# Expert weights split into fp32r parts, moving past stationary tokens, in a hybrid diffusion step

## The reference, cut to what matters

```python
hidden = jax.nn.silu(jnp.einsum('nd,edf->nef', xt, w1)) * jnp.einsum('nd,edf->nef', xt, w3)
y = jnp.einsum('nef,efd->nd', hidden * combine[:, :, None].astype(hidden.dtype), w2)
```

## Time and profile before

| | |
|---|---|
| median of 3 runs | 1863.83 us (1862.94 to 1865.37) |
| the profiled execution's own time | 1864.37 us |
| its span in the trace | 1862.6 us |
| mean granted TensorE clock over the span | 0.91 |
| TensorE matmul busy | 1517.4 us, 81% |
| VectorE busy | 744.2 us, 40% |
| ScalarE busy | 426.4 us, 23% |
| GpSimd busy | 214.2 us, 11% |
| router of layer 0, first instruction to `tok_i` | 739.3 to 760.3 us |
| experts of layer 0, first gather to last down | 760.7 to 996.3 us |
| router of layer 1 | 1522.3 to 1543.2 us |
| experts of layer 1 | 1543.7 to 1806.1 us |

### The profile page before, as it was taken

The page is one execution under the profiler, slowest core; times in us unless marked ns, Lnnn a source line. Parts: engine busy times, 40 slices in busy tenths (PEclk is TensorE's granted clock), DMA queues, the critical chain, the costliest instruction groups (busy, mean ns, idle before and its releaser), DMA issues. The chain is left out here.

```text
span 1862.6 us, 25715 instructions
## 1 busy us (share of the span) xinstructions
PE 1517.4 (81%) x9767; PEld 1213.7 (65%) x9768; DVE 744.2 (40%) x1388; ACT 426.4 (23%) x832; POOL 214.2 (11%) x166
## 2 busy tenths in 40 slices
PE   4699999656899997599993199989997867999970
PEld 1588888555576444477882199987884446777760
DVE  0312122266477343311114835428993752111118
ACT  1311212242343011011112312125552111101113
POOL 1000000112000032100003400010000321100016
PEclk9899999878999998699997599999998977999995
DMA  7576755701000901559994032220006225877763
GB/s 270 176 238 211 242 182 160 171 12 31 1 1 1 296 34 54 170 173 342 354 352 168 23 94 69 80 60 1 1 1 183 102 91 198 280 260 256 269 215 146
DMA packets 190509, 277.82 MB, mean 149 GB/s; under 512 B 12888, under 2 KB 130352, under 8 KB 190416
## 3 DMA queue, kind: packets, MB, share of 16 engines
q1 hardware_dynamic: 180032, 239.15, 39.0%
q0 software_dynamic: 9520, 34.24, 5.3%
q10 hardware_dynamic: 864, 3.15, 0.4%
HBM read 246.90 MB, written 34.85 MB: 151 GB/s over the span
## 5 line engine op out<-in xcount | busy, mean ns | idle before, releaser
L480 PEld LDWEIGHTS psum<-in_parts 128*128 128x128 f32 x3360 | 411.3, 191 | 59.2 <-issue 59.2
L480 PE MATMUL psum<-in_parts 128*128 128x258 f32 (+1 forms) x3360 | 421.2, 286 | 25.3 <-PEq L322 25.3
L773 PE MATMUL psum<-layer 128*128 128x512 f32 x400 | 173.7, 594 | 2.7 <-PEq L698 2.7
L1777 PEld LDWEIGHTS psum<-layer 128*128 128x128 f32 x1280 | 145.7, 192 | 15.2 <-issue 7.6
L1777 PE MATMUL psum<-layer 128*128 128x128 f32 x1280 | 146.5, 275 | 6.7 <-DVE layer L1983 6.7
L1777 PEld LDWEIGHTS psum<-layer,arena 128*128 128x128 f32 x1152 | 137.9, 200 | 13.2 <-issue 6.7
L1777 PE MATMUL psum<-layer,arena 128*128 128x128 f32 x1152 | 138.6, 284 | 5.3 <-DVE layer L1983 3.6
L773 PEld LDWEIGHTS psum<-layer 128*128 128x128 f32 x400 | 75.8, 191 | 95.2 <-issue 95.2
L566 DVE COPY arena<-psum 128x258 f32<-128x258 f32 (+1 forms) x70 | 29.7, 425 | 240.8 <-PE psum L480 240.8
L1168 PE MATMUL psum<-layer 128*128 128x320 f32 (+1 forms) x384 | 114.2, 434 | 5.0 <-PEq L1358 1.7
L1265 ACT ACTIVATE layer<-psum,layer 128x640 f32<-128x640 f32 (+1 forms) x120 | 84.3, 705 | 118.5 <-DVE layer L1211 118.5
(11 more groups left out here) (298 smaller groups left out, 1872.7 us busy)
## 6 DMA issues: line engine op xcount, KB each, us to landing
arena<-in_moe_w SPq DMA_DIRECT2D x48, 1024.0 KB, 9.3
layer<-in_moe_w SPq DMA_DIRECT2D x48, 1024.0 KB, 8.7
in<-in_ada_w SPq DMA_DIRECT2D x40, 1024.0 KB, 5.2
y_rows<-layer SPq DMA_DIRECT2D x64, 256.0 KB, 8.5
in<-in_ev_w_in SPq DMA_DIRECT2D x15, 1032.0 KB, 7.6
in<-in_od_w_in SPq DMA_DIRECT2D x11, 1024.0 KB, 5.1
start<-in_ada_w SPq DMA_DIRECT2D x8, 1024.0 KB, 16.6
arena<-mod_rows SPq DMA_DIRECT2D x16, 512.0 KB, 7.7
```

The costliest lines, as they stand in the source:

```text
L480: last = T.matmul(bank(g % W_BANKS)[:, 0:cw], a, b[:, k], start=(k == 0 and m == 0), stop=(k == KD - 1 and m == 2))
L773: last = T.matmul(bank(g % 4), feats[k][:, t * P:(t + 1) * P], wout[:, k, j * BANK:(j + 1) * BANK], start=(k == 0), stop=(k == kt - 1))
L1777: last = T.matmul(dst[:, (2 * f + m) * P:(2 * f + m + 1) * P], weights[m][:, k, f * P:(f + 1) * P], xT[:, k, :], start=(k == 0), stop=(k = ...
```

## The change

The host stores w1 and w3 of an expert beside each other and by partition, so each of the 128 partitions is one run of 16 KB, and w2 as one run of 8 KB. There are three slots for the arriving weights; SP loads the w1/w3 of expert e+3 (in two halves) once up(e) has ended, and w2 of e+3 behind the store of e. Each weight is split: ScalarE copies the high part, rounded to fp32r, to a place of its own; the low part is written over the raw words, by VectorE for w1/w3 and by GpSimd for w2. Turned tokens are split in the same way, ScalarE for the high part and VectorE for the low part, out of PSUM.

In `up` the tokens are stationary and 512 columns of w1 and w3 together move; for each of the eight k there are three products, high by high, high by low and low by high: 24 matmuls into bank 2. The hidden values then have tokens on the partitions, so after silu and the multiplication TensorE turns them (`turn_h`, two transposes), ScalarE and VectorE split them, and `down` is 12 matmuls of 512 columns. The tokens of a further chunk are turned and split one ahead, in two halves through bank 3, and the chunk uses the split weights of its expert. The loop body holds six experts instead of two.

Expert 0 is prepared in `router`: ScalarE makes three high parts (before and behind its two exponentials), and GpSimd three low parts of 128x2048. `router` also loads the weights of experts 1 and 2, where it loaded those of expert 1. The token lists have two more columns, and `experts` starts with three gathers (experts 0 and 1 and the first further chunk), all turned before the first `up`. The four loads for `combine` are issued behind up(13). The arena is allocated in another way, at the same places. The diff is cut to its core: most lines taken away are left out.

```diff
+HK, W13, W2 = KD // 2, 2 * KD * FF, 2 * D
+LOW13_AT = [BIG + 12 * D, R, R + W13]
+LOW2_AT = [BIG + 12 * D + W13, BIG + 12 * D + W13 + W2, R + 2 * W13]
+HIGH13_AT = [BIG + n * W13 for n in range(3)]
+HIGH2_AT = [R + 2 * W13 + W2 + n * W2 for n in range(2)]
+REST = R + 2 * W13 + 3 * W2
...
+def load13(sp, s, w13):
+    for h in range(2):
+        sp.dma_start(raw13(s, h), w13[:, h * HK:(h + 1) * HK]).then_inc(up_in[s][h], 16)
+def load2(sp, s, w2):
+    sp.dma_start(raw2(s), w2).then_inc(dn_in[s], 16)
...
-sp.dma_start(E13[0], I["moe_w1"][i, 0].rearrange("(k p) f -> p k f", p=P)).then_inc(up_in[0], 16)
-sp.dma_start(E13[1], I["moe_w3"][i, 0].rearrange("(k p) f -> p k f", p=P)).then_inc(up_in[0], 16)
-sp.dma_start(E2, I["moe_w2"][i, 0].rearrange("(f p) n -> p f n", p=P)).then_inc(dn_in[0], 16)
+load13(sp, 0, I["moe_w13"][i, 0])
+load2(sp, 0, I["moe_w2"][i, 0])
+load2(sp, 1, I["moe_w2"][i, 1])
...
+    load13(sp, 1, I["moe_w13"][i, 1])
+    load13(sp, 2, I["moe_w13"][i, 2])
+    load2(sp, 2, I["moe_w2"][i, 2])
+@block.gpsimd
+def _(pool):
+    for h in range(2):
+        pool.wait_ge(high_w, h + 1)
+        nc.gpsimd.tensor_tensor(low13(0, h), raw13(0, h), whole(high13(0, h)), ALU.subtract).then_inc(low_w, 1)
+    pool.wait_ge(high_w2, 1)
+    nc.gpsimd.tensor_tensor(low2(0), raw2(0), whole(high2(0)), ALU.subtract).then_inc(low_w2, 1)
...
 @block.scalar
 def _(act):
+    act.wait_ge(up_in[0][0], 16)
+    A.copy(high13(0, 0), raw13(0, 0)).then_inc(high_w, 1)
     act.wait_ge(nm, 1)
     A.activation(pg, pg, ACT.Exp).then_inc(ex, 1)
     act.wait_ge(nm, 2)
     A.activation(pe_, pe_, ACT.Exp).then_inc(ex, 1)
+    act.wait_ge(up_in[0][1], 16)
+    A.copy(high13(0, 1), raw13(0, 1)).then_inc(high_w, 1)
+    act.wait_ge(dn_in[0], 16)
+    A.copy(high2(0), raw2(0)).then_inc(high_w2, 1)
...
-expert(0, 0, True)
-expert(1, 1, True)
-with eng.Fori(1, HALF) as pair:
-    expert(pair * 2, 0, False)
-    expert(pair * 2 + 1, 1, False)
+def one(e, n):
+    expert(e, n % 3, n % 2, (e - n % 3) // 3 if isinstance(e, int) else None)
+one(0, 0)
+with eng.Fori(0, 2) as six:
+    for j in range(1, 7):
+        expert(six * 6 + j, j % 3, j % 2, six * 2 + j // 3)
+for e in range(NE - 3, NE):
+    one(e, e)
...
+def expert(e, s, b, v):
     done = entry(sp, 2, e)
...
+    more = not (isinstance(e, int) and e >= NE - 3)
+    sp.wait_ge(up_s, e + 1)
+    sp.wait_ge(o_up, done)
     if more:
...
+        load13(sp, s, W13S[bass.ds(e + 3, 1)].rearrange("a p k f -> p (a k) f"))
+    if isinstance(e, int) and e == NE - 3:
+        g2, gb = COMBINE
+        for c in range(2):
+            sp.dma_start(g2[:, c, :].rearrange("p (k m) -> p k m", k=KD), mod_row(i, 5, c)).then_inc(g2_in[i], 16)
+        sp.dma_start(gb[:, 0, :], I["ln2_g"][i].partition_broadcast(P)).then_inc(ln2_in[i], 16)
+        sp.dma_start(gb[:, 1, :], I["ln2_b"][i].partition_broadcast(P)).then_inc(ln2_in[i], 16)
...
+sp.wait_ge(y_a, e + 1)
+sp.wait_ge(y_d, e + 1)
+sp.dma_start(chunk_rows(e), yb[:, b, :]).then_inc(y_out[b], 16)
...
     sp.wait_ge(o_y, done)
...
+    load2(sp, s, W2S[bass.ds(e + 3, 1)].rearrange("a p f n -> p (a f) n"))
...
+def gather(row, col, out, done):
+    nc.gpsimd.tensor_copy(rows[:, row:row + 1], tok_i[:, col:col + 1] if isinstance(col, int) else tok_i[:, bass.ds(col, 1)])
     pool.drain()
...
+def expert(e, s, b, v):
+    pool.wait_ge(turned, e * 2 + 2)
+    gather(b, e + 2, xg[:, b, :], xg_in[b])
+    if not last_of(e):
+        pool.wait_ge(high_w2, e + 2)
+        nc.gpsimd.tensor_tensor(low2((s + 1) % 3), raw2((s + 1) % 3), whole(high2(1 - b)),
+                                ALU.subtract).then_inc(low_w2, 1)
+    def chunk(q):
+        pool.wait_ge(o_turned, q * 2 + 2)
+        gather(2, q + (NE + 1), xg_o, o_in)
     further(pool, e, chunk)
...
+for b in range(2):
+    gather(b, b, xg[:, b, :], xg_in[b])
+gather(2, NE, xg_o, o_in)
 loop(pool, expert)
+for b in range(2):
+    pool.wait_ge(xg_in[b], 8 * (NE + 2))
+pool.drain()
 pool.wait_ge(o_out, entry(pool, 2, NE - 1) * 16)
...
+def turn_half(src, h, dst, done):
+    for k in range(HP):
+        last = T.transpose(dst[:, k * P:(k + 1) * P], src[:, (h * HP + k) * P:(h * HP + k + 1) * P], ident)
+    last.then_inc(done, 1)
+def up(s, x_high, x_low, half, done):
     for k in range(KD):
...
+        half(k)
+        high, low = high13(s, k // HP)[:, k % HP], low13(s, k // HP)[:, k % HP]
+        for m, (a, w) in enumerate(((x_high, high), (x_high, low), (x_low, high))):
+            last = T.matmul(bank(2), a[:, k, :], w, start=(k == 0 and m == 0), stop=(k == KD - 1 and m == 2))
+    last.then_inc(done, 1)
+def turn_h(done):
+    for f in range(2):
+        last = T.transpose(bank(2)[:, f * P:(f + 1) * P], gate[:, f * P:(f + 1) * P], ident)
+    last.then_inc(done, 1)
+def down(b0, s, b, low_ready, done):
+    first, second = high2(b), low2(s)
+    for f in range(2):
+        for w in (first, second):
+            for j in range(2):
+                T.matmul(bank(b0 + j), hh[:, f, :], w[:, f, j * BANK:(j + 1) * BANK],
+                         start=(f == 0 and w is first), stop=False)
+    low_ready()
+    for f in range(2):
+        for j in range(2):
+            last = T.matmul(bank(b0 + j), hl[:, f, :], first[:, f, j * BANK:(j + 1) * BANK], start=False, stop=(f == 1))
+    last.then_inc(done, 1)
+def expert(e, s, b, v):
+    def half(k):
+        if k % HP == 0:
+            pe.wait_ge(x_low, e * 2 + (k // HP + 1))
+            pe.wait_ge(low_w, e * 2 + (k // HP + 1))
+    up(s, xh, xl, half, up_s)
+    pe.wait_ge(xg_in[1 - b], (e + (2 + b)) * 8)
+    for h in range(2):
+        turn_half(xg[:, 1 - b, :], h, bank(h), turned)
     pe.wait_ge(hid_s, e + 1)
...
+    turn_h(h_turned)
+    pe.wait_ge(low_w2, e + 1)
+    pe.wait_ge(h_high, e + 1)
+    if not (isinstance(e, int) and e == 0):
         pe.wait_ge(y_a, e + 0)
         pe.wait_ge(y_d, e + 0)
...
+    down(4, s, b, lambda: pe.wait_ge(h_low, e + 1), y_s)
+    def chunk(q):
+        def half(k):
+            if k % HP == 0:
+                pe.wait_ge(o_xl, q * 2 + (k // HP + 1))
+        up(s, xh_o, xl_o, half, o_up)
+        pe.wait_ge(o_in, (q + 2) * 16)
+        turn_half(xg_o, 0, bank(3), o_turned)
         pe.wait_ge(o_hid, q + 1)
...
+        turn_h(o_ht)
+        pe.wait_ge(o_xl, q * 2 + 3)
+        turn_half(xg_o, 1, bank(3), o_turned)
+        pe.wait_ge(o_hh, q + 1)
+        pe.wait_ge(o_ya, q + 1)
+        pe.wait_ge(o_yd, q + 1)
+        down(6, s, b, lambda: pe.wait_ge(o_hl, q + 1), o_y)
     further(pe, e, chunk)
...
+pe.wait_ge(xg_in[0], 16)
+for h in range(2):
+    turn_half(xg[:, 0, :], h, bank(h), turned)
+pe.wait_ge(o_in, 16)
+turn_half(xg_o, 0, bank(3), o_turned)
+pe.wait_ge(o_xl, 1)
+turn_half(xg_o, 1, bank(3), o_turned)
 loop(pe, expert)
...
+def x_of(e):
+    for h in range(2):
+        act.wait_ge(turned, e * 2 + (h + 1))
+        A.copy(x_half(xh, h), turned_x(h)).then_inc(x_high, 1)
+def x_of_further(q, h):
+    act.wait_ge(o_turned, q * 2 + (h + 1))
+    A.copy(x_half(xh_o, h), turned_x(3)).then_inc(o_xh, 1)
+def split13(e, s, v, h):
+    act.wait_ge(up_in[s][h], (v + 1) * 16)
+    A.copy(high13(s, h), raw13(s, h)).then_inc(high_w, 1)
+def expert(e, s, b, v):
+    s1, v1 = (s + 1) % 3, v + (s == 2)
+    if not last_of(e):
+        split13(e + 1, s1, v1, 0)
+        act.wait_ge(dn_in[s1], (v1 + 1) * 16)
+        A.copy(high2(1 - b), raw2(s1)).then_inc(high_w2, 1)
     act.wait_ge(up_s, e + 1)
...
+    A.activation(gate, bank(2)[:, 0:FF], ACT.Silu).then_inc(silu_s, 1)
+    x_of(e + 1)
+    act.wait_ge(h_turned, e + 1)
+    A.copy(hh, turned_h).then_inc(h_high, 1)
+    if not last_of(e):
+        split13(e + 1, s1, v1, 1)
     act.wait_ge(y_s, e + 1)
...
+    act.wait_ge(y_out[b], (e + (2 - b)) * 8)
     A.copy(yb[:, b, 0:BANK], bank(4)).then_inc(y_a, 1)
...
+    def chunk(q):
         act.wait_ge(o_up, q + 2)
...
+        A.activation(gate, bank(2)[:, 0:FF], ACT.Silu).then_inc(o_silu, 1)
+        x_of_further(q + 1, 0)
+        act.wait_ge(o_ht, q + 1)
+        A.copy(hh, turned_h).then_inc(o_hh, 1)
+        x_of_further(q + 1, 1)
+        act.wait_ge(o_y, q + 2)
+        act.wait_ge(o_out, (q + 1) * 16)
+        A.copy(yb_o[:, 0:BANK], bank(6)).then_inc(o_ya, 1)
+        act.wait_ge(o_ya, q + 2)
+        act.wait_ge(o_yd, q + 2)
         act.dma_start(chunk_rows(q + NE), yb_o).then_inc(o_out, 16)
     further(act, e, chunk)
...
+def x_of(e):
+    for h in range(2):
+        dve.wait_ge(x_high, e * 2 + (h + 1))
+        V.tensor_tensor(x_half(xl, h), turned_x(h), whole(x_half(xh, h)), ALU.subtract).then_inc(x_low, 1)
+def x_of_further(q, h):
+    dve.wait_ge(o_xh, q * 2 + (h + 1))
+    V.tensor_tensor(x_half(xl_o, h), turned_x(3), whole(x_half(xh_o, h)), ALU.subtract).then_inc(o_xl, 1)
+def split13(e, s, h):
+    dve.wait_ge(high_w, e * 2 + (h + 1))
+    V.tensor_tensor(low13(s, h), raw13(s, h), whole(high13(s, h)), ALU.subtract).then_inc(low_w, 1)
+def expert(e, s, b, v):
+    if not last_of(e):
```

(20 more changed lines are left out.)

266 lines of the change are left out of this document (95 added, 171 removed).

## The result

The changed kernel took 1855.06 us (median of 13 runs, 1846.62 to 1859.34), the one before 1864.39 in the runs beside it. The ratio is 0.995, interval 0.9939 to 0.9961: 9 us faster, where 41 were forecast, yet 1 us inside the upper end of the range of 1798 to 1856. The profiled execution took 1855.64 us with a span of 1853.8, so it lies 32 us above the sum of the prediction, and those 32 us are what has to be found.

The account below looks back on a forecast made before the run. TensorE was taken to bound, transfers keeping up with nothing to spare. Experts -74.7, router +26.2, start +7.0 and end +0.6 sum to -40.9 us from 1864.4, giving 1823.5; forecast 1823, range 1798 to 1856.

Parts of the forecast that it names:

- the router: In `router`, GpSimd's three subtractions make VectorE's small steps wait: 13.1 us, twice, +26.2 us in all.
- the start: Start of `experts`: first `up` waits for the third gather; expert 0's silu moves by +3.5 us, twice +7.0.
- the plain gap: Between `up` and `down` of an expert: `down` starts 2.15 us after silu starts, behind x copies and h copy.
- the transfers: Rival: weight transfers bound the experts, 11.8 us for each at 354 GB/s; 1830 to 1846 us, chance 0.2.
- the clock in every gap: Rival: TensorE's clock falls in the gap before `down`, one in six giving +11 us, 1834 us; chance 0.1.
- further chunks: In `experts`, each further chunk of an expert costs 10.0 us in place of 14.6; six such chunks are counted.
- `up` and `down`: In `experts`, 24 and 12 products of 512 columns at 0.216 us each: `up` 5.2 us, `down` 2.6 us.
- the 0.15 for the port: Added to the expert period because VectorE and GpSimd subtractions exclude each other: 10.15 becomes 10.3 us.
- The splits: In `experts`, splits fit the 10.15 us period: ScalarE 8.3, VectorE 7.5, GpSimd 6.5; mutually exclusive subtractions take 9.1.
- The slack: Room left in the expert period beside the mutually exclusive VectorE and GpSimd subtractions: 1.1 us.
- The end: Behind expert 15's silu: `down` starts 1.25 us later and is 1.1 shorter; with the store, +0.3 us each.

## Why the prediction was off

The signs were right, and so were the mechanisms of the router, the start and the plain gap; the time was 32 us too low. That the measured time lies in the range at all is luck: its upper end had been drawn for rivals (the transfers, the clock in every gap) that did not come about, and what did happen was not among them.

**The step that failed: further chunks.** "Tokens are turned and split ahead, so a chunk is `up` 5.2, the same gap with half the x work between `turn_h` and `down` (2.2), `down` 2.6: 10.0." The tokens of *this* chunk are ahead, but in the gap TensorE turns those of the *next* one. I had counted these turns and copies and put the wait for their gather at nothing, though it comes even when no expert needs them soon. I never placed that gather on GpSimd's queue, where it stands behind the w2 subtraction and its own copy. The gap was 3.6 to 5.8 us, `down` lost its clock in two of the six, and a chunk cost 13.2 on average: +19 us. With the gather ahead of the subtraction the gap is 2.2 in four of them, which cost 10.6, the forecast plus the dearer products. So of the 19 us 13 go with the gather's move, some 4 are the dearer products, and the rest is the wait that two chunks keep. Which chunks lose the clock, and how many, changes from trace to trace: four of six with the turn in two pieces, behind gaps of about the same length.

**`up` and `down`: a term too small.** I had a measured upper bound, 0.234 us from twice the 256-column row, and took 0.216, reasoning from `down`'s old records, which are of another form. A record of `up` lasts 0.39 us, so the 24 in 5.81 us start (5.81 - 0.39) / 23 = 0.236 us apart. That is the upper bound; the price goes by columns. `up` took 5.85 us to the silu where I had 5.2 and 0.2, +0.45, and `down` up to the next `up` 2.95 where I had 2.6, +0.35. The gap came out 0.26 shorter than forecast, and the 0.15 for the port was not needed. In sum some +0.35 for each of 30 steps, +10 us.

**The gap.** 1.9 against 2.15, in the order that I gave: x copies, h copy, `down`. Right.

**The splits.** "The order works out" was right, with GpSimd starting 0.3 us ahead of the silu and ending 4.6 behind it, and VectorE's second half stretched from 2.29 to 3.06 us. The slack was about right as well: with GpSimd 2.2 us later the kernel is slower than before.

**The router.** +13.1 was forecast, the first gather came 12.5 us later against the router's start. Three steps of 0.18 us became 4.21, 4.46 and 4.42, which is 12.55 more. The mechanism is the one given, shown by taking the subtractions away.

**The start.** +3.5 in each layer together with the router's 13.1 makes +16.6; measured 16.3 and 16.5. The third gather is what `up` waits for. **The end**: from S(15) to the next router, and to the end of the program, it is 1.5 and 0.9 us more instead of 0.3 each. Another 1.1 us lie ahead of the first router, less than the 6.6 us by which its start differs between traces. With these the 32 us are complete: 29.6 in the experts, 1.8 behind them, 1.1 ahead, less 0.4 at the starts.

**The rivals.** The transfers do not bound. The rule of the Trainium skill, "DMA: Bandwidth & Descriptors", section "Where 436 GB/s comes from", would have held an expert at an estimated 11.7 us; 379 GB/s over 120 us, and 384 over 50 us with 1 KB rows, speak against it as a ceiling for a core alone. The section names no row length; "whatever the row length" was my reading of it. The rival of the clock was half right: not in all gaps, but in two of six chunks, and in this kernel only behind waits for the gather. The window around the worst one (columns as in the earlier trace rows) has the granted clock at 0.66 of full, between its two levels 1.2 and 2.4 GHz, with transposes and no matmuls of weights in the pause:

```profile
1744.00:1754.00 10.00, 6.51 (x22) 5.20 (x22) 2.14 (x4) 1.83 (x4) 0.96 (x1) 0.66 0.94 338
```

The gaps of 1.9 us, which hold ten transposes, kept the clock at 1.00 from 860 to 980.

## What to carry to other kernels

When an engine that was 99% busy gets cheaper work, list for each other engine's queue what stands ahead of what the fast engine will ask for next: here a gather behind a subtraction cost about as much (13 us) as all the mis-sized products together (some 14). Test the new bound by leaving work out: that a third of `up` could go and a plain step fell by 0.6 us at most told more than the busy shares. Ask as well which transfer the end of the shortened work releases, and what is under way then: the shorter `up` put a weight load on top of the gather for which it then waited. And a piece of work moved off the path has to be priced with the queue that it lands in: the same turn gained nothing in one place and 14 us in another.
